# Two rows of x loaded within the second branch group, with other rooms and another order of splits

## The reference

```python
h = rms_norm(x, norm_mix_pre[l])
z = h @ w_in[l]
...
ya = oa @ w_branch_a[l]
...
merged = gates[:, :, 0] * ya + gates[:, :, 1] * yx + gates[:, :, 2] * yp
x = x + rms_norm(merged @ w_out[l], norm_mix_post[l])

h = rms_norm(x, norm_ffn_pre[l])
f = (jax.nn.silu(h @ w_ffn_gate[l]) * (h @ w_ffn_up[l])) @ w_ffn_down[l]
x = x + rms_norm(f, norm_ffn_post[l])
```

## Time and profile before

| | |
|---|---|
| Time, median of 3 runs | 785.55 us (785.29 to 786.08) |
| Profiled execution: its own time | 785.32 us |
| Profiled execution: its span | 783.1 us |
| PE busy | 768.6 us (98%) |
| PEld / DVE / ACT / POOL busy | 683.7 / 600.8 / 390.7 / 101.8 us |

### The profile page before, as it was taken

The page is one execution under the profiler, slowest core; times in us unless marked ns, Lnnn a source line. Parts: engine busy times, 40 slices in busy tenths (PEclk is TensorE's granted clock), DMA queues, the critical chain, the costliest instruction groups (busy, mean ns, idle before and its releaser), DMA issues.

```text
span 783.1 us, 12284 instructions
## 1 busy us (share of the span) xinstructions
PE 768.6 (98%) x4814; PEld 683.7 (87%) x4814; DVE 600.8 (77%) x669; ACT 390.7 (50%) x614; POOL 101.8 (13%) x151
## 2 busy tenths in 40 slices
PE   8999999999999999999998999999999999999997
PEld 7888778777877899989976899999999999888885
DVE  6656566677866788889954588888888888999897
ACT  7823445444336345555523564445444445675462
POOL 5211102334184000000001110000011110000002
PEclk9999999999999999999999999999999999999999
DMA  8958913115723233466572013333333346214102
GB/s 299 322 174 292 192 54 108 54 55 137 212 81 95 68 108 108 142 235 190 188 246 74 3 54 109 108 107 107 107 107 107 107 134 215 107 54 163 52 1 108
DMA packets 76105, 101.53 MB, mean 130 GB/s; under 512 B 3856, under 2 KB 63008, under 8 KB 76064
## 3 DMA queue, kind: packets, MB, share of 16 engines
q1 hardware_dynamic: 71312, 89.95, 34.9%
q0 software_dynamic: 4288, 10.49, 5.5%
q10 hardware_dynamic: 464, 0.53, 0.2%
HBM read 96.75 MB, written 12.60 MB: 140 GB/s over the span
## 4 chain that ended last, share of the span: by engine, by line
PE 46%; DVE 7%; DMA 3%; issue 1%; SPq 1%; ACT 1%; DVEq 0%; POOLq 0%; POOL 0%; ACTq 0%
PE pair L2229 46%; DVE late_op_lo L1638 1%; DMA br_raw<-in_w_branch_a 1%; DMA g_ffn_pre_b<-in_norm_ffn_pre 1%; DVE br_out L1692 1%; DMA raw<-in_w_out 1%; PE pair L2236 0%; DVE wo_lo L517 0%; DVE br_op_lo L1638 0%; DVE gates L1695 0%; DVE br_T_lo L1644 0%; DVE gates L1627 0%; DVE part L1624 0%; DVE mrg_lo L1631 0%; DVE br_out L1688 0%
## 5 line engine op out<-in xcount | busy, mean ns | idle before, releaser
L2229 PE MATMUL pair<-hT_hi,w_hi 128*128 128x512 f32 x240 | 98.1, 409 | 0.0
L2229 PE MATMUL pair<-hT_hi,w_lo 128*128 128x512 f32 x240 | 93.8, 391 | 0.0
L2229 PE MATMUL pair<-hT_lo,w_hi 128*128 128x512 f32 x240 | 93.6, 390 | 0.0
L2229 PE MATMUL pair<-T_hi,op_hi 128*128 128x256 f32 x320 | 90.6, 283 | 0.0
L2229 PE MATMUL pair<-T_lo,op_hi 128*128 128x256 f32 x320 | 90.6, 283 | 0.0
L2229 PE MATMUL pair<-T_hi,op_lo 128*128 128x256 f32 x320 | 90.6, 283 | 0.0
L517 DVE TENSOR_TENSOR w_lo<-raw,w_hi 128x1024 fp32r<-128x1024 f32 x44 | 59.8, 1360 | 24.3 <-ACT w_hi L504 24.2
L2229 PE MATMUL pair<-B_hi,op_hi 128*128 128x256 f32 x240 | 67.9, 283 | 0.0
L2229 PE MATMUL pair<-B_lo,op_hi 128*128 128x256 f32 x240 | 67.9, 283 | 0.0
L2229 PE MATMUL pair<-B_hi,op_lo 128*128 128x256 f32 x240 | 67.9, 283 | 0.0
L504 ACT ACTIVATE w_hi<-raw 128x1024 fp32r<-128x1024 f32 x44 | 46.3, 1055 | 39.2 <-PE pair L2229 31.1
(11 more groups left out here) (313 smaller groups left out, 2177.8 us busy)
## 6 DMA issues: line engine op xcount, KB each, us to landing
raw<-in_w_in SPq DMA_DIRECT2D x42, 512.0 KB, 4.9
raw<-in_w_ffn_up SPq DMA_DIRECT2D x22, 512.0 KB, 4.8
raw<-in_w_ffn_gate SPq DMA_DIRECT2D x22, 512.0 KB, 4.3
W<-in_w_ffn_down SPq DMA_DIRECT2D x8, 1024.0 KB, 5.0
br_S<-in_w_branch_a POOLq DMA_DIRECT2D x6, 1024.0 KB, 12.2
raw<-in_w_out SPq DMA_DIRECT2D x8, 512.0 KB, 4.2
raw<-in_w_ffn_down SPq DMA_DIRECT2D x6, 512.0 KB, 4.6
br_raw<-in_w_branch_a SPq DMA_DIRECT2D x5, 512.0 KB, 4.5
```

The lines of the kernel that those rows point to most:

```text
L2229: ins = pe.matmul(dst, a, b, start=first and n == 0, stop=last and n == 2, skip_group_check=onto)
```

## The change

The diff touches memory places, waits and the order of steps; no arithmetic is changed.

- A room `br_third` (120 and 124 KB) is made for operand n = 2, which before went to `br_op[2]`. ACT's waits change with it: operand 2 waits for no tile, operand 3 waits for the last pooling tile.
- `wo_hi[6]`, `wo_lo[6]` move from 196 and 200 KB to 192 and 196 KB, `wo_lo`/`wo_hi` of slab 7 from 88 and 92 to 92 and 200 KB. Slab 6 no longer waits for `br_blocks` 8, slab 7 waits for `mrg_split` 7 instead of 8, and its DVE step for `br_blocks` 8.
- SP loads rows 0 and 1 of x and `g_post_b` after product 7 (`br_done` 8), ahead of the slabs of `w_out`; rows 2 and 3 after the last product; `g_ffn_pre_b` after the last merge (`br_merged` 8).
- `br_block_out` is cut in a read and a merge, so that slab 7 is split between the two for the last block.
- ACT's and DVE's lists for the stage are written in another order.

```diff
@@ -206,6 +205,7 @@
     br_op = late_op[2:3] + late_op[0:2]
     br_op.append([sb(f"br_op3_{m}", 176 + 4 * n, [P, 4, 2 * P], F32R)[:, :, :] for n, m in enumerate(("hi", "lo"))])
+    br_third = [sb(f"br_third_{m}", 120 + 4 * n, [P, 4, 2 * P], F32R)[:, :, :] for n, m in enumerate(("hi", "lo"))]
...
-    out_at = [(80, 84), (72, 76), (40, 48), (44, 52), (56, 64), (60, 68), (196, 200), (88, 92)]
+    out_at = [(80, 84), (72, 76), (40, 48), (44, 52), (56, 64), (60, 68), (192, 196), (92, 200)]
...
             elif kind == "out" and n == 6:
-                eng.wait_ge(br_blocks, 8)
                 eng.wait_ge(br_split, 2 * OPS)
             elif kind == "out":
-                eng.wait_ge(mrg_split, 8)
+                eng.wait_ge(mrg_split, 7)
...
+        def br_operand(n):
+
+            return br_third if n == 2 else br_op[n % 4]
...
             for n in range(2, 2 * OPS):
                 load_branch(n)
+            sp.wait_ge(br_done, OPS + 1)
+            for t in range(2):
+                sp.dma_start(x1[:, t, :], x[P * t:P * t + P, :]).then_inc(x_loaded[t], 16)
+            sp.dma_start(g_post_b[:, :], row_bcast(g_mix_post)).then_inc(gain_loaded["post"], 16)
             sp.wait_ge(br_split, 2 * OPS - 2)
             for c in range(late_chunk + 2, last_out + 1):
                 load_chunk(c)
             sp.wait_ge(br_done, 2 * OPS)
-            sp.wait_ge(mixed_last, 4 * len(BRANCH) - BY_DMA)
-            for t in range(TT):
+            for t in range(2, TT):
                 sp.dma_start(x1[:, t, :], x[P * t:P * t + P, :]).then_inc(x_loaded[t], 16)
-            sp.dma_start(g_post_b[:, :], row_bcast(g_mix_post)).then_inc(gain_loaded["post"], 16)
+            sp.wait_ge(br_merged, 4 * len(BRANCH))
             sp.dma_start(g_ffn_pre_b[:, :], row_bcast(g_ffn_pre)).then_inc(gain_loaded["ffn_pre"], 16)
...
                 if n == 0:
                     act.wait_ge(late_done, OPS * len(LATE))
-                elif n < 3:
-                    act.wait_ge(tile_full, step_end[A0 + n - 1])
+                elif n in (1, 3):
+                    act.wait_ge(tile_full, step_end[A0 + n // 2])
...
+            br_operand_lo(12)
+            br_operand_lo(13)
             br_block_out(1, "C11")
...
+            br_block_read(1, "C12")
+            dve.wait_ge(br_blocks, 4 * len(BRANCH))
+            out_lo(7)
+            br_block_merge(1, "C12")
             merged_lo(7)
-            out_lo(7)
```

More of the change, by code:

```diff
@@ L370, in encoder_block @@
         br_hi, br_split, br_done = sem("br_hi"), sem("br_split"), sem("br_done")
-        br_kept_ready, br_blocks, mixed_last = sem("br_kept_ready"), sem("br_blocks"), sem("mixed_last")
-        br_mixed = [sem(f"br_mixed{i}") for i in range(2)]
+        br_kept_ready, br_blocks, br_merged = sem("br_kept_ready"), sem("br_blocks"), sem("br_merged")
         ops_hi, ops_split, product_done = sem("ops_hi"), sem("ops_split"), sem("product_done")
@@ L961, in _ @@
                 .then_inc(late_t_made, 1)
[L963 to L967, removed]
             for n in range(NORM_MIX, NORM_POST):
@@ L1247, in _ @@
             br_operand_hi(6)
-            br_operand_hi(7)
             merged_hi(0)
             br_keep(0, "U3")
+            br_operand_hi(7)
             br_operand_hi(8)
             br_operand_hi(9)
+            merged_hi(1)
+            merged_hi(2)
             br_operand_hi(10)
-            merged_hi(1)
             br_keep(1, "U1")
             br_operand_hi(11)
-            merged_hi(2)
+            merged_hi(3)
+            out_hi(1)
             br_operand_hi(12)
-            merged_hi(3)
             br_keep(1, "U2")
             br_operand_hi(13)
-            out_hi(1)
             out_hi(2)
+            br_keep(1, "U3")
+            merged_hi(4)
             out_hi(3)
-            merged_hi(4)
-            br_keep(1, "U3")
             out_hi(4)
+            merged_hi(5)
             out_hi(5)
-            merged_hi(5)
             merged_hi(6)
             out_hi(6)
+            out_hi(7)
             merged_hi(7)
-            out_hi(7)
             done += KT
@@ L1689, in br_block_out, with br_block_merge @@
                 ins.then_inc(br_blocks, 1)
+            def br_block_merge(g, c):
+                b = 4 * g + BLOCK_ORDER.index(c)
+                out = br_out[b % 4][:, :, :]
                 dve.wait_ge(br_blocks, b + 1)
@@ L1692, in br_block_out @@
                 dve.tensor_tensor(out, out, br_part(late_gates, b), ALU.mult).then_inc(br_gated, 1)
-                if b >= BY_DMA:
-                    dve.wait_ge(br_gated, b + 1)
-                    dve.tensor_tensor(br_part(gates, b), br_part(gates, b), out, ALU.add).then_inc(mixed_last, 1)
+                dve.wait_ge(br_gated, b + 1)
+                dve.tensor_tensor(br_part(gates, b), br_part(gates, b), out, ALU.add).then_inc(br_merged, 1)
+            def br_block_out(g, c):
+                br_block_read(g, c)
+                br_block_merge(g, c)
             def out_lo(k):
@@ L1902, in _ @@
                     br_token_lo("T2")
-            br_token_lo("T1")
             br_operand_lo(1)
+            br_operand_lo(2)
             for t in steps[NS - 1]:
                 merge(t)
-            br_operand_lo(2)
+            br_token_lo("T1")
             br_operand_lo(3)
@@ L1915, in _ @@
             br_operand_lo(6)
-            br_operand_lo(7)
             merged_lo(0)
             br_block_out(0, "C22")
+            br_operand_lo(7)
+            br_block_out(0, "C21")
             br_operand_lo(8)
-            br_block_out(0, "C21")
             br_operand_lo(9)
             br_block_out(0, "C12")
+            merged_lo(1)
+            merged_lo(2)
             br_operand_lo(10)
-            merged_lo(1)
             br_operand_lo(11)
-            merged_lo(2)
+            merged_lo(3)
+            out_lo(1)
+            br_operand_lo(12)
+            br_operand_lo(13)
             br_block_out(1, "C11")
-            br_operand_lo(12)
-            merged_lo(3)
-            br_operand_lo(13)
-            out_lo(1)
             out_lo(2)
+            br_block_out(1, "C22")
+            merged_lo(4)
             out_lo(3)
-            merged_lo(4)
-            br_block_out(1, "C22")
+            br_block_out(1, "C21")
             out_lo(4)
-            br_block_out(1, "C21")
+            merged_lo(5)
             out_lo(5)
-            merged_lo(5)
-            br_block_out(1, "C12")
             merged_lo(6)
             out_lo(6)
+            br_block_read(1, "C12")
+            dve.wait_ge(br_blocks, 4 * len(BRANCH))
+            out_lo(7)
+            br_block_merge(1, "C12")
             merged_lo(7)
-            out_lo(7)
             done += KT
```

20 lines of the change are left out of this document (6 added, 14 removed).

## The result

The changed kernel takes 780.3 us (median of 10 runs, 779.17 to 783.19); the kernel before, run beside it on the same chip, 785.42 us (783.05 to 787.48). The ratio is 0.9938, 95% interval 0.992 to 0.9956. Forecast were 779.6 us in a range of 778.0 to 782.2 and a gain with a chance of 0.92: it held. The profiled execution took 779.71 us with a span of 777.9 us, against 785.32 and 783.1 before.

A forecast was written before the change was run, and what follows sets the result against it. PE, busy 98%, was taken as the bound. The turn 4.3 us sooner plus 1.6 for the clock, with 0.1 for slower transposes, made 6.0 off the median 785.55: 779.6 us, range 778.0 to 782.2.

The forecast's parts named there:

- What bounds the kernel: Whole span: PE, busy 98%; its longest wait, 3.7 us for `y` at the turn, ends a chain behind `g_ffn_pre_b`.
- Step 1: Operand 2's room and first reordering, up to 372.74 us: nothing for the end, at most 1.0 us.
- Step 2: DVE's new list from 372.74 us: added waits of 1.2 and 0.4 us, row t = 0 starting at 388.9.
- The order of splits gains nothing up to there: Up to row t = 0 of the output projection: start at 388.9, as before at 389.01.
- Step 3: Output slabs: no PE wait at slab 6, hardly one at slab 7; row 0 ends at 399.8, before 402.1.
- not yet on the path: Out row 0's gain of 2.2 us only brings PE to the turn at 409.3 instead of 411.6.
- Step 4: `g_ffn_pre_b` issued alone at 399.5, taking 3.9 us; transposes at 411.1 instead of 415.42, 4.3 us sooner.
- The clock: Behind the turn: stays at 2.4 GHz after 1.8 us of wait; rival that it falls: 781.2 us, chance 0.12.
- The early loads push the output weights: Rival at O2 and P3: two half slabs land 1.5 us later, delaying all slabs; 781.1 us, chance 0.12.
- The wait goes wholly: Rival at the turn: lone load takes 3.1 us, PE finds `y` nearly ready; 777.8 to 778.5 us, chance 0.08.
- It does not do what it says: Rival at the turn: DVE's own list holds it near 415; 784.5 to 785.6 us, chance 0.04.
- slower: Rival at O2: second half slab lands at 389.3, P3 waits 6.4 us longer; 787.6 us, chance 0.04.

The follow-up runs named there:

- e1: Kernel before the change with only the new places of the loads, lists and rooms as before: 781.53 us, ratio 0.9946.
- e2: Changed kernel with the loads put back at their old place, new lists and rooms kept: 788.7 us, ratio 1.0043.
- e3: Changed kernel with a second copy of `g_ffn_pre_b` loaded early into its own room for rows 0 and 1: 778.03 us, ratio 0.9902.
- e8: Changed kernel with slabs 1 and 2 split later, behind operand 12 and block C22, load as in the change: 779.32 us, ratio 0.9921.
- e5: Changed kernel with the last block C12 merged ahead of slab 7 on DVE instead of behind it: 779.14 us, ratio 0.9923.
- e6: Changed kernel with the loads of slabs 2 and 3 issued ahead of the early x rows and `g_post_b`: 781.36 us, ratio 0.9943.
- e4: Changed kernel with dummy DVE products ahead of row 0's `y`: one product 784.08 us, ratio 0.998; two products 784.35 us, ratio 0.9989.
- e7: Changed kernel with the early second gain copy and slabs 1 and 2 split behind operand 12 and block C22: 776.53 us, ratio 0.9891.

## Why the prediction was right, and where it was off

*What bounds the kernel.* Right: PE, and on it the turn behind the load. e1 (the loads alone bring 4.4 us), e2 (without them the lists lose 3.4) and e3 (with the load off the chain the wait is gone) show it from both sides.

*Step 1, worth nothing.* Right at its own rows: the step behind C12 of group 0 starts at 372.70 on DVE, before at 372.74, P6 waits 0.21 instead of 0.51, P4 0.30 (forecast 0.5), and the first wait for C22 is gone.

*Step 2.* Right in its places: DVE waits 1.13 us at slab 1 (forecast 1.2), P7 0.46 (0.5), slab 2 waits 0.60 (0.4), row t = 0 starts at 389.16 (388.9). P3's wait was put too short: 0.70 us, at 386.21 instead of 385.9 to 386.0. One term is right without its working: 3.1 + 2 x 1.75 from 371.2 bring the three early loads to 377.8, not to 380.0, and then slab 2 would not have waited. Measured is 380.1 (`g_post_b`, issued at 372.18, took 7.9), since the last operand loads were still on the queue: the one issued at 370.76 took 5.5. And "The order of splits gains nothing up to there" holds only with the early loads: without them (e2) it gains 0.65 us at row t = 0. Nor is this the best order: e8 takes both DVE waits away and the turn comes 1.45 us sooner, since DVE's list also sets when the last merge, and so the load, goes.

*Step 3.* Right: no waits for slabs 6 and 7; PE was ready for the turn 2.0 us sooner than before, forecast 2.3. That this gain was "not yet on the path" is shown by e5: it gives 1.18 us of it back and is 1.1 us of span faster.

*Step 4.* The release was right (399.37, forecast 399.5). The size of the lone load was the mis-sized term: 4.4 us where 3.9 was taken, inside the bounds of 3.1 and 5.1. It is no accident of one run: 4.1 to 4.5 in the seven kernels that load it alone, 4.5 in e1, e5 and e8. Behind it come some 0.4 us between the landing and DVE's start, where 0.1 was put. Together 0.8; the earlier release gives 0.1 back: 411.8 instead of 411.1. The row of x (3.1) was the wrong neighbour to lean on for a gain row written to 128 partitions. The Trainium skill's page "DMA: Bandwidth & Descriptors", section "Anatomy of one DMA — SWDGE (gpsimd) path", has its figures for another issuing path; the estimate of 3.2 us from them is too short for this load on SP's queue.

*The clock.* The forecast said it stays high at 1.8 us, and gave the other case 0.12. In the profiled execution it stayed, at 2.04 us. Over the executions of the changed kernel it did not always: seven have spans of 777.4 to 778.7 at a mean granted clock of 0.998 or 0.999, three of 779.2 to 781.4 at 0.997. With the same kind of wait, e6 has three of 777.4 to 778.2 at 0.998 to 0.999 and three of 780.9 to 781.1 at 0.996, and e8 three of each. By the mean clocks, then, the rival is a case that happens in about three to five of ten executions, and 0.12 was too small for it. That the clock fell at the turn in those unprofiled executions is inferred; seen in a trace it is in e6 and e8. A fall is worth 1.6 us, so spans like 780.7 and 781.4 hold something else too: e6's profile (780.9) has, beside the fall, the stage 2 us later.

The clock does not explain the median, which is 0.7 over the forecast: the two executions around it have spans of 778.4 at 0.999. In the profile the turn is the 0.7 us late of step 4, so the span fell by 5.2 instead of 5.9; the time fell by 0.4 more than the span (1.8 us lie around it, before 2.2), and the rest of the median is the spread of executions without a fall, 777.4 to 778.7, in which the price of the early loads at P3 (nothing to 1.4 us) is one part that can be seen.

*The other rivals.* "The early loads push the output weights": real, and of no fixed size. The change's row t = 0 starts 0.80 us later than e2's, and P3's wait is anything from nothing to 1.41 us in five kernels, beside the 1.5 of the rival. In the old order, with slabs 2 and 3 ahead of the reading of C22, P3 waits 1.48 (e1). "The wait goes wholly": no, but e3 shows what it would give, 776.1 of span. "It does not do what it says" and "slower" fell: slab 2's data was in at 383.15, four microseconds ahead of the point from which the second decides.

## What to carry to other kernels

When a load is the last link of a chain, look at three times apart: when it is released, how many loads stand ahead of it on its queue, and how long it takes alone. Moving five loads away made 9.5 us into 4.4; what was left was a later release and the load itself, and a list that cures PE's small waits can put that release later and lose (e2), so follow each new order to the instruction that lets the load go. Where a wait of two to three microseconds remains ahead of dense matmuls, its price is itself and, in some executions, a stretch at half clock (1.6 us here): take it away wholly, rather than shorten it. And before a wait of some tenths is priced from one pair of profiles, look at it in every kernel that should have it.

## What the runs showed of the hardware

The fall of TensorE's clock behind a wait is not a matter of the wait's length alone. After 1.97 us (e6) and 2.15 (e8) it fell, after 2.04 (the change) it did not; after 3.25, 3.67, 4.3 and 9.7 it fell in the one profile of each; behind 1.18, 1.26, 1.29, 1.41 and 1.48 in none. Nor does it fall at a fixed distance: in e6 it falls as PE starts again (PEclk is 0.70 from 413 to 414 us, the turn starts at 413.17), in the kernel before PEclk is still 1.00 from 415 to 416 us, in the transposes, and the matmuls slow down from 416.6 on. The price of a fall is even: from turn to turn 13.45 to 13.48 us in the kernel before, both forms of e4, e6 and e8, against 11.80 to 11.86 in the change, e1, e3, e5 and e7, so 1.6 us. The kernel before seems to have both kinds too: of 46 executions 36 have spans of 782.2 to 787.0 at 0.995 to 0.997, ten of 780.3 to 782.5 at 0.998 or 0.999. Without a wait at the turn the times lie close together, within 1.1 us in e3 and 0.9 in e7, 1.2 in e1 and 1.6 in e5. The Trainium skill's page "TensorE: Matmul & The Clock Gate", section "🎯 Why this matters for your kernels", warns of idle gaps between bursts of matmuls and names one length from which they cost; the traces agree on the effect, but here waits shorter than that length lowered the clock too (1.97 and 2.15 us). What decides between two executions with like waits stays open.

A gain row written to 128 partitions (512 KB) took 4.1 to 4.5 us with nothing ahead of it, in seven kernels, where a load of x of the same size took 3.1 (in the kernel before). DVE began 0.4 to 0.5 us after the landing in six kernels, e2 among them, and after 0.1 in the kernel before and e5; what makes the difference is open.
